# The first norm of a two-layer backbone: x in two halves between the modulation tiles, ten tiles on TensorE, squares added by VectorE

## The reference

```python
def rms_norm(x, g):
    xf = x.astype(F32)
    y = xf * lax.rsqrt(jnp.mean(xf * xf, axis=-1, keepdims=True) + EPS)
    return (y * g.astype(F32)).astype(x.dtype)

def _modulate(h, g, m, k):
    return (rms_norm(h, g) * (1 + m[:, :, 3 * k + 1]) + m[:, :, 3 * k]).astype(h.dtype)

def _half_ffn(h, g, m, k, w1, w3, w2):
    y = swiglu(_modulate(h, g, m, k), w1, w3, w2)
    return h + (0.5 * m[:, :, 3 * k + 2] * y).astype(h.dtype)
```

## Time and profile before

| | us |
|---|---|
| median of three timed runs | 2786.47 |
| the profiled execution | 2784.83 |
| its span | 2783.1 |
| TensorE busy | 2675.1 (96%) |
| VectorE busy | 2056.2 (74%) |
| ScalarE busy | 1176.3 (42%) |
| GpSimd busy | 390.2 (14%) |

### The profile page before, as it was taken

The page is one execution under the profiler, slowest core; times in us unless marked ns, Lnnn a source line. Parts: engine busy times, 40 slices in busy tenths (PEclk is TensorE's granted clock), DMA queues, the critical chain, the costliest instruction groups (busy, mean ns, idle before and its releaser), DMA issues.

```text
span 2783.1 us, 40131 instructions
## 1 busy us (share of the span) xinstructions
PE 2675.1 (96%) x15624; PEld 2512.6 (90%) x15624; DVE 2056.2 (74%) x3184; ACT 1176.3 (42%) x1860; POOL 390.2 (14%) x312
## 2 busy tenths in 40 slices
PE   5999999999988999999999999999999989999999
PEld 5999999998976899999999999999997775788898
DVE  7887878774558587878777877787878667666674
ACT  3233333346447644332323523242436866533342
POOL 3111111110012521111111211100022410211000
PEclk8999999999999999999999999999999999999999
DMA  9888989621120047889897589874522110378453
GB/s 347 209 228 248 274 252 267 169 67 54 59 62 1 1 143 203 245 224 281 229 274 212 137 221 258 248 214 131 165 69 83 61 46 1 114 201 235 145 165 125
DMA packets 161691, 464.13 MB, mean 167 GB/s; under 512 B 13281, under 2 KB 14433, under 8 KB 160609
## 3 DMA queue, kind: packets, MB, share of 16 engines
q1 hardware_dynamic: 87200, 247.65, 26.3%
q0 software_dynamic: 56448, 146.81, 24.3%
q10 hardware_dynamic: 17856, 67.12, 6.8%
HBM read 459.43 MB, written 148.90 MB: 219 GB/s over the span
## 4 chain that ended last, share of the span: by engine, by line
PE 78%; DVE 11%; DMA 5%; ACT 3%; issue 3%; POOL 0%; ACTq 0%; SPq 0%; DVEq 0%; POOLq 0%
PE banks L698 11%; PE banks L702 11%; PE banks L700 11%; PE banks L786 9%; PE banks L788 9%; PE banks L787 9%; DMA raw<-sums 4%; PE banks L705 3%; PE banks L709 3%; PE banks L707 3%; DVE banks L2019 1%; DVE tmp L2292 1%; PE banks L1233 1%; DVE wl L2086 1%; DVE wl L2014 1%
## 5 line engine op out<-in xcount | busy, mean ns | idle before, releaser
L1362 ACT ACTIVATE wh<-raw 128x1024 fp32r<-128x1024 f32 (+2 forms) x194 | 181.8, 937 | 611.8 <-PE banks L702 458.7
L2019 DVE SCALAR_TENSOR_TENSOR banks<-mraw,scb 128x1024 f32<-128x1024 f32 x240 | 304.9, 1270 | 11.6 <-DMA mraw<-in_wmn 7.9
L2014 DVE TENSOR_TENSOR wl<-raw,wh 128x1024 fp32r<-128x1024 f32 (+2 forms) x216 | 234.3, 1085 | 95.5 <-ACT wh L1362 93.2
L1427 ACT ACTIVATE wh<-raw 128x512 fp32r<-128x512 f32 (+1 forms) x210 | 161.6, 774 | 326.6 <-DMA raw<-sums 156.7
L698 PE MATMUL banks<-hh,wh 128*128 128x384 f32 x1056 | 270.4, 337 | 9.3 <-DVE wl L2014 9.0
L786 PE MATMUL banks<-xh,wh 128*128 128x384 f32 (+1 forms) x796 | 258.0, 324 | 12.8 <-DVE wl L2086 12.7
L702 PE MATMUL banks<-hh,wl 128*128 128x384 f32 x1056 | 269.9, 336 | 0.0
L700 PE MATMUL banks<-hl,wh 128*128 128x384 f32 x1056 | 269.7, 336 | 0.0
L788 PE MATMUL banks<-xh,wl 128*128 128x384 f32 (+1 forms) x796 | 256.6, 322 | 0.0
L787 PE MATMUL banks<-xl,wh 128*128 128x384 f32 (+1 forms) x796 | 256.5, 322 | 0.0
L698 PE MATMUL banks<-xh,wh 128*128 128x384 f32 x880 | 230.7, 343 | 21.4 <-DVE xl L2284 12.0
(11 more groups left out here) (427 smaller groups left out, 6225.5 us busy)
## 6 DMA issues: line engine op xcount, KB each, us to landing
raw<-sums SPq DMA_DIRECT2D x140, 512.0 KB, 6.0
sums<-in_w POOLq DMA_DIRECT2D x88, 768.0 KB, 8.5
mraw<-in_wmn ACTq DMA_DIRECT2D x120, 512.0 KB, 5.7
a<-in_w SPq DMA_DIRECT2D x70, 512.0 KB, 4.3
sums<-in_w POOLq DMA_DIRECT2D x22, 1536.0 KB, 8.8
sums<-sums POOLq DMA_DIRECT2D x44, 768.0 KB, 9.6
raw<-in_w SPq DMA_DIRECT2D x80, 384.0 KB, 4.3
raw<-in_w SPq DMA_DIRECT2D x52, 512.0 KB, 3.9
```

The costliest lines, as they stand in the source:

```text
L1362: act.activation(wh[slot][:, 0:nk * P], raw[slot][:, 0:nk * P], ACT.Copy).then_inc(hi_done, 1)
L1427: act.activation(W_HI[slot_of(name, last)], W_SRC[name], ACT.Copy).then_inc(w_hi, 1)
L2014: dve.tensor_tensor(wl[slot][:, 0:nk * P], raw[slot][:, 0:nk * P], wh[slot][:, 0:nk * P].bitcast(F32), ALU.subtract).then_inc(lo_done, 1)
L2019: return dve.scalar_tensor_tensor(B67[:], tile, 1.0, scv[:, s, :], ALU.mult, ALU.mult, accum_out=out)
```

## The change

SyncE loads par, the first two weight tiles and scb0, then the minis in eight groups with x in two halves behind the first and the second group. The scale tiles (8 to 15) come first, then the shift tiles. TensorE makes ten minis (8 to 12, then, behind the sum of the squares, 0, 1, 2, and once rstd is there 4 and 5), VectorE six (13, 14, 15, 3 ahead of the norm; 6 and 7 inside it, between the fourth `scaled` and `rest(0)`). ScalarE writes eight squares into eight buffers, with no wait between them; VectorE adds them to one sum, so the sum over partitions is two matmuls and not four. The bias is added in three batches: scale, shift of chunks 0 to 3, shift of chunks 4 to 7; ScalarE's xh(0) and xh(4) wait for the second and third. The splits of the first two weight tiles move to the front of ScalarE's and VectorE's programs. The gate tiles are issued behind weight tiles 2 and 3, each once the minis in its place are read. GpSimd's chain of DMAs waits for the last mini.

```diff
-PE_MINI = (1, 3, 5, 7, 9, 11, 13)
-DVE_MINI = (0, 2, 4, 6, 8, 10, 12, 14, 15)
-MINI_GROUPS = ((0, 1, 2), (3, 4, 5, 6), (7, 8, 9, 10), (11, 12, 13), (14, 15))
+PE_MINI = (8, 9, 10, 11, 12, 0, 1, 2, 4, 5)
+DVE_MINI = (13, 14, 15, 3, 6, 7)
+MINI_GROUPS = ((8, 9, 13), (10, 11, 14), (12, 15), (3, 0), (6, 1), (7, 2), (4,), (5,))
...
+            def load_gate_minis():
+                for q in range(2):
+                    sp.wait_ge(mini_mm, 2 + q)
+                    sp.wait_ge(mini_dot, (9, 14)[q])
+                    sp.dma_start(gmini[q][:], dr["wmn"][16 + 4 * q:20 + 4 * q].rearrange("t p n -> p t n")).then_inc(gmini_landed, 16)
+                sp.dma_start(wdt[:], dr["wdt"]).then_inc(gmini_landed, 16)
...
+            for q, js in enumerate(MINI_GROUPS):
+                for j in js:
+                    src = dr["wmk"][PE_MINI.index(j)] if j in PE_MINI else dr["wmn"][j]
+                    sp.dma_start(mini[j][:], src).then_inc(mini_landed[q], 16)
+                if q < 2:
+                    half_k = slice(4 * q, 4 * q + 4)
+                    sp.dma_start(x[:, half_k, :], dr["x"][:, half_k, :]).then_inc(x_landed[q], 16)
...
             for j in PE_MINI:
-                if j == 11:
-                    pe.wait_ge(con_landed, 16)
+                if j == 0:
+                    pe.wait_ge(x_landed[0], 32)
                     norm_sums(0, SEGS)
+                if j == 4:
+                    pe.wait_ge(rstd_ready, 1)
...
                 for j in range(KC):
+                    if n == 0 and j % 4 == 0:
+                        act.wait_ge(mini_dot, (9, 14)[j // 4])
                     act.wait_ge(v_ready, 8 * n + j + 1)
...
+            def add_square(j):
+                dve.wait_ge(sq_done, j + 1)
+                if j > 1:
+                    dve.wait_ge(ssq_acc, j - 1)
+                dve.tensor_tensor(ssq[:], ssq[:], squares[j][:], ALU.add).then_inc(ssq_acc, 1)
...
+            def shift_batch(q):
+                dve.wait_ge(mini_mm, 2 + q)
+                dve.wait_ge(mini_dot, (8, 13)[q])
+                first_bias(4 * q, (3, 2)[q], 4).then_inc(mini_dot, 1)
+                dve.wait_ge(mini_dot, (9, 14)[q])
+
+            def first_between(q):
+                if q == 0:
+                    shift_batch(0)
+                    first_dots(6, 9)
+                    first_dots(7, 11)
+                if q == 1:
+                    shift_batch(1)
...
-            add_squares(0, T)
+            pool.wait_ge(mini_landed[len(MINI_GROUPS) - 1], 16 * len(MINI_GROUPS[-1]))
```

More of the change, by code:

```diff
@@ L277, in pr @@
             return par[:, PCOL[n][0]:PCOL[n][1]]
-        mini = [at(f"mini{j}", [P, D], XH + j * D) for j in range(2 * KC)]
-        gmini = [at("gmini0", [P, 4, D], H + 4 * D), at("gmini1", [P, 4, D], H)]
+        mini = [at(f"mini{j}", [P, D], (H if j < KC else XH - KC * D) + j * D) for j in range(2 * KC)]
+        gmini = [at(f"gmini{q}", [P, 4, D], H + 4 * q * D) for q in range(2)]
+        squares = [ssq, sq[0], sq[1], tmp[0], tmp[1], tmp[2], tmp[3], rstd]
         scb0 = at("scb0", [P, 2, D], HID + 2 * HC * T - 3 * T)
@@ L623, in load_ffn @@
                             load(t0 + 2 * i + 1, src[1], KC)
+                        if (f, g, i) == (0, 0, 1):
+                            load_gate_minis()
                     row2 = KC * W2_ROW[f, g]
@@ L633, in load_ffn @@
                             load_a2(f, g + 1, 0)
+            def load_gate_minis():
[4 more added lines that the diff above has]
+                sp.dma_start(wdt[:], dr["wdt"]).then_inc(gmini_landed, 16)
             sp.dma_start(par[:], dr["par"]).then_inc(par_landed, 16)
+            for s in range(2):
+                sp.dma_start(raw[s][:, 0:D], dr["w13"][s]).then_inc(raw_landed[s], 16)
             sp.dma_start(scb0[:], dr["ccb"]).then_inc(scb_landed, 16)
[L637 to L651, removed]
+            for q, js in enumerate(MINI_GROUPS):
[6 more added lines that the diff above has]
+                if q == 0:
+                    sp.dma_start(con[:], dr["con"]).then_inc(x_landed[0], 16)
             load_ffn(0)
@@ L749, in norm_sums @@
                 pe.wait_ge(ssq_acc, 7 * (n + 1))
+                if n == 0:
+                    for a, b, _s in segs:
+                        mm = pe.matmul(NP[:, a:b], cst("ones"), ssq[:, a:b], start=True, stop=True)
+                    mm.then_inc(norm_sum, 1)
+                    return
                 for a, b, _s in segs:
@@ new lines, in shift_batch @@
+            def shift_batch(q):
[4 more added lines that the diff above has]
+            def first_between(q):
+                if q == 0:
+                    shift_batch(0)
[3 more added lines that the diff above has]
+                    shift_batch(1)
+            chain(dve.memset(eps[:], EPS))
@@ L2860, in _ @@
+            split_lo(0, 0, KC)
+            split_lo(1, 1, KC)
+            dve.wait_ge(scb_ready, 1)
+            first_dots(13, 0)
+            for j in range(1, 4):
+                add_square(j)
+            first_dots(14, 2)
+            for j in range(4, KC):
+                add_square(j)
+            first_dots(15, 4)
+            first_dots(3, 6)
             dve.wait_ge(par_landed, 16)
             dve.wait_ge(mini_mm, 1)
-            dve.wait_ge(mini_dot, 2 * len(DVE_MINI))
-            pairs = G[0][:, 0:4 * KC].rearrange("p (t s) -> p t s", s=2)
@@ L2864, in _ @@
-            for js, src in ((slice(1, 14, 2), pairs), (slice(0, 15, 2), M), (slice(15, 16), M)):
-                n_ = len(range(16)[js])
-                chain(dve.tensor_tensor(M[:, js, :], src[:, js, :], pr("bmod")[:, js].unsqueeze(2).to_broadcast([P, n_, 2]),
-                                        ALU.add))
+            dve.wait_ge(mini_dot, 8)
+            chain(first_bias(KC, 5, KC))
             prep(0)
-            norm(0, SEGS, lambda s: None)
+            norm(0, SEGS, first_between)
```

62 lines of the change are left out of this document (33 added, 29 removed).

## The result

The changed kernel took 2793.89 us (median of 20 runs, 2785.42 to 2807.29), the kernel before 2787.11 beside it (20 runs, 2780.5 to 2790.54): a ratio of 1.0025, 95% interval 1.0016 to 1.0033. It is slower by about 7 us; the prediction was 2785.1, with 2790.0 as its upper end. Run again on another chip the ratio was 1.0035 (1.0022 to 1.0048). The profiled execution took 2795.98 us (span 2794.2, mean granted clock 0.991; before 0.990).

What follows compares the result with a forecast made beforehand. Bound taken: a chain of waits (first minis landing, VectorE's 18 dots, the norm) up to TensorE's first large product at 57.09 us. Sum: -5.8 + 2.7 + 1.7 = -1.4 against 2786.47, so 2785.1 us; range 2779.5 to 2790.

Steps and rivals of the forecast that it cites:

- The time to the first product: TensorE's start on its first large product: 51.3 us where it was 57.09, so 5.8 us won.
- the formula: Landing times of the first loads: 3.3 + 1.225 n us, with n counted in minis of 512 KB.
- the lower level: TensorE's clock at 1.2 GHz during minis, 3.45 us each; the upper level is 2.4 GHz.
- the new wait of VectorE: In the norm, after four `scaled`: VectorE waits from 41.4 us for TensorE's mini 2 at 44.35.
- rival C: Minis behind the sum of the squares run at 1.9 us: start 48.4, 8.7 won, 2782.2 us; chance 10%.
- what is late next: Behind the first product: scb, slowed by the second gate load, lands at 70.4, silu 72.3, after TensorE's 69.6.
- a stall of 2.7: TensorE waiting for scb's silu behind its first large product: 2.7 us, bounds 0 to 5.5.
- 1.7 for the clock: Behind TensorE's stop of 5.1 us the granted clock falls to 0.50 for some 3 us: 1.7 us lost.
- rival D: scb and second gate load meet, but worse: stall 6.9, clock 2.4, +3.5 us, 2790.0 us; chance 18%.
- TensorE waiting later for sums: A sign in the profile after that would make the prediction wrong; no size was given.
- the dots with the gate tiles: Gate tiles land about 71 to 73 us, needed by VectorE's dots at 74.7: just hidden.
- GpSimd's chain ahead of the second norm: GpSimd's DMAs start at 36.8 and not 31.3 us, leaving 8 of 15.9 us to spare: hidden.

Runs made afterwards that it cites:

- e1: The changed kernel with scb's load issued right behind rstd's Exp and not behind xh(7): ratio 0.9981 to the kernel before.
- e5: The changed kernel unaltered, run again on another chip: ratio 1.0035 to the kernel before.
- e8: The changed kernel with scb loaded right behind rstd's Exp and GpSimd's chain started behind the fourth group of minis: ratio 0.9996 to the kernel before.
- e10: The changed kernel with scb loaded right behind rstd's Exp and the second gate load issued behind weight tile 4: ratio 0.9983 to the kernel before, 2785.6 us.
- e11: The changed kernel with scb loaded right behind rstd's Exp, measured once more: ratio 0.9990 to the kernel before, 2785.28 us.
- e2: The changed kernel with GpSimd's DMA chain started when the fourth group of minis has landed, not the last: ratio 1.0002 to the kernel before.
- e6: The changed kernel with the second gate load and wdt issued behind weight tile 4: ratio 1.0009 to the kernel before, 2789.85 us.
- e4: The kernel before with three more tiles in `wmk` that nothing reads, shifting later tensors in DRAM: ratio 1.0004 to the kernel before.
- e9: The kernel before with ScalarE copying scb onto itself twice ahead of its silu: ratio 1.0015 to the kernel before.
- e3: The kernel before with GpSimd's DMA chain started only when the last mini has landed: ratio 0.9982 to the kernel before.
- e7: The kernel before with scb's load issued right behind rstd's Exp: ratio 0.9991 to the kernel before unaltered.
- e12: The kernel before with scb's load issued right behind rstd's Exp, measured once more: ratio 0.9987 to the kernel before unaltered, 2784.06 us.

## Why the prediction was wrong

**The time to the first product was right.** Predicted 51.3, measured 51.96 (and 51.3 to 52.0 in e1, e5, e8, e10 and e11). The two groups and the two halves of x on TensorE's path landed 0.6 to 1.0 us behind the formula (the last minis, which nothing on the path waits for, by up to 2); the minis behind the sum of the squares took 17.07 / 5 = 3.41 us each, the lower level, as taken; rstd was there at 38.1 (predicted 37.1); the new wait of VectorE was 2.53 us. 5.1 us won, 5.8 predicted. The two executions e2 and e6 show that rival C can happen in part: there the first product came at 49.83 and 49.45, where C, its sum put right (41.8 + 5.3 + 1.1 is 48.2), has 48.2.

**The step that failed is "what is late next".** It gave scb 8.0 us, a stall of 2.7 and 1.7 for the clock, and of the other neighbour it said "GpSimd's DMA chain lies beside it as it did before". Three things are wrong in that. And the sum has no term at all for the rounds that read the sums; more on that below.

First, the size: scb took 9.2 us, the stop grew by 4.6 (6.04 - 1.42), and the low clock of 6.05 us behind it took 3.0. Set against the start (5.1) and the shorter low clock behind the first product (1.5 us lost there where it was 2.5), that is 4.6 + 3.0 - 5.1 - 1.0 = 1.5 us lost, and the split is 1.3 late. The mechanism is rival D's, which was to decide from a stall of 4.1 us; 4.6 was measured. The 8.0 had been taken as the middle between 5.3 and 10.8 (by its own terms, 5.3 and half of 11.6, the upper one is 11.1), with no row in which two such loads lie together. And the first product does not end at 75.36, where ScalarE gets its buffer back, but at 76.31 (77.73 less the wait of 1.42): the stop before was 1.42 us and not 2.4. The forecast's 5.1 us of stop are 4.1 by this measure, and 6.04 were measured.

Second, the neighbour. I took the second gate load as what makes scb slow. But e4 and e9 had 8.6 and 9.3 us with no gate load near, and e6 still 7.5 without it; e10 against e11 shows no gain in moving it, though e10 pays for that elsewhere. With scb behind the norm, the six executions in which GpSimd's transfer was issued 1.3 us or more ahead of it had 7.5 to 9.3 us, the two with less than that 4.8 and 5.3. The gate load may add up to 1.7 us in the new order (9.2, 8.8 and 8.9 against 7.5), but it isn't needed. That it is the transfer is read from which loads lie together in eight executions; of edits, only e3 moves the transfer alone, in the old order, where scb was quick already. The changed kernel with that one transfer held back until scb has landed was not run. In the kernel before it was issued 0.68 us ahead:

```profile
65.84 1.26 POOL L2916 DMA_DIRECT2D sums<-in_w  x1 [11.62 <-issue]
```

With its own issue at 66.52, its profile showed the good case. The rates fit: from scb's issue to 68 us and from there to 70 the core's DMAs moved 26 and 159 GB/s in e4 (busy for 65% and 96%), and 74 and 340 (53% and 83%) in the kernel before. So it looks as if the slow DRAM to DRAM transfer was served first in e4 and scb in the kernel before. The changed order issues scb 3.6 us earlier, into the middle of the transfer issued at 57.50, each time that it was profiled. The Trainium skill (DMA: Bandwidth & Descriptors, Queues, rings and completion order) has each DMA engine go round-robin between the queues that have work. The trace of the changed kernel agrees in kind: scb and the transfer both finish late, after 9.2 and 15.8 us, where in e10, with neither scb nor the second gate load beside it, the same transfer took 7.6. I had applied the rule to SyncE's queue alone.

Third, the kernel before seems to pay this toll too, in some of its executions: e4, whose program is the same but for tiles that nothing reads, showed it. e3, which moves the transfer behind scb (0.7 us), and e7 and e12, which move scb away, are 0.9982, 0.9991 and 0.9987 of it, but only e3's interval ends below 1. How often it happens no run shows. That the one profile of a kernel with two ways to go may have drawn the good one was no part of my range.

**Is the late scb the cause?** For the sign, taking it away is enough: the one edit that does so turns 1.0025 and 1.0035 into 0.9981 and 0.9990, and the intervals do not touch. The same edit in the old order (e7, e12) is worth a quarter of that. Of the gain the profiles show 6.2 us at the split (131.1 against 137.3: restart 3.5 us earlier, the low clock gone). But it isn't shown to be the only cause: e6 and e2 took 6 to 9 us off the changed kernel by the ratios, with scb still at 7.5 and 8.9 us and stops of 4.3 and 5.8. Nor can the other low stretches of the changed kernel be put down to the late scb. The one at 140 us follows a stop of 2.88 us that the kernel before has too, with the same low stretch behind it, as have e7 and e12, where scb is early; e1, e8 and e11 have the stop and stay at the full clock. The one at 318 us is missing in e5 and there in e12 (near 321).

**What stays open** is the later part, and it decides the forecast: with only the 1.5 us of the failed step, the prediction's own sum would have given 2788.0, inside its range; the measured 2793.89 lies outside by what comes after 137 us. The prediction put that part at nothing, without a row, and named "TensorE waiting later for sums" as a sign that it is wrong; that sign is there. By the medians the change costs 6.8 us; 1.3 are there at 137 us in one execution, and -1.3 in another (e5). The rest is in the rounds that read the sums, where TensorE's waits come to 18.6 and 15.2 us in the changed kernel, 12.7 before. The chain's start (against it e3 and e8, for it e2), the DRAM places (e4) and the stop itself (e9: 7.2 us of such waits after the longest stop of all) don't explain it by themselves. e10 had 17.3 us of them with no late scb, though with late gate tiles, and ended 10.9 us behind before; e11 had 12.3. They differ from execution to execution of one kernel, and fourteen profiles do not say by what. Nor is it clear why a lead of 5 us at 131 us (e11 against e12: 131.1 and 136.1), which is still there at the end of the two profiled executions (2780.5 and 2785.8), isn't seen in the medians (2785.28 and 2784.06). No run here holds the later waits fixed.

**What was hidden as predicted.** The first squares and rstd; `shift_batch(1)`; the dots with the gate tiles, which began at 76.12, right behind tile 2's rest and with no wait; GpSimd's chain ahead of the second norm, which answers to the earlier trace rows:

```profile
544.99 1.40 POOL L2945 COPY ssq<-sq 128x768 f32<-128x768 f32 x1 [7.55 <-ACT sq L1497]
```

Early by 7.6 us where 8 were predicted and 15.9 stood before.

## What to carry to other kernels

A step that is started earlier moves every transfer behind it as well: look up each one's neighbours at its *new* time, on every queue, GpSimd's among them, and not only the neighbour that the change itself moves. If a small load stands on the path and its data and buffer are there long before, issue it early: the rebuilt start was worth nothing that shows without it, and with it no more than the old start with the same edit (e1 and e11 against the changed kernel: 10 to 15 us by the ratios; e7 and e12 against the kernel before: about 3, with intervals that end at 1.0002). A cure that moves another load needs the same look: e6 and e10 made VectorE wait for the gate tiles. And where the profiled time of a load hangs on which of two issues comes first by under a microsecond, take both times into the range.

## What the runs showed of the hardware

- A load of 1 MB behind the norm took 4.8 and 5.3 us, or 7.5 to 9.3 where GpSimd's queue had been given its transfer more than a microsecond earlier. Between 0.7 us ahead (5.3) and 1.3 us (8.6) lies the whole step, on two executions. GpSimd's instruction that issues the transfer lasted 1.26 us: in the first it was still running when scb was issued, in the second it had just ended. That this order decides fits all eight, but was not tested, and e7's early load, 0.5 us behind a transfer and with other loads about it, took 7.2, so the bound is not a rule.
- With stops of 3.7 to 8.4 us of TensorE behind its first large product a low granted clock came every time (3.4, 6.8 or 10.2 us long, begun within the stop in five of the six), and with the 1.42 us at the same place never. Its length does not follow that of the stop alone: 6.04 us went with 6.8 us of it, 5.71 with 3.4. A stop of 2.88 us some 60 us later was followed by a low stretch in ten of the thirteen executions that have it, and in e1, e8 and e11 by none; nothing here says why.
- The price of a stop is not only itself: in e9 7.0 us more of stop made 9.8 us at the split, 2.4 of them by the low clock behind it.
- Matmuls with 2 columns stayed at the lower level for 17 us in a row (80 of them, 17.07 us). In two of the eight executions of the new order (e2 and e6) the first of them behind the sum of the squares ran at the upper one, until 39 us.
- Profiled executions of nearly the same work ended at 2776.4 and 2785.8 us (e7 and e12), 2778.2 and 2780.5 (e1 and e11), 2794.2 and 2789.0 (after and e5). A difference of 5 us between two single profiles says nothing about the kernel; the same instruction at 76 or 137 us does, within 0.6 us at the split (130.99 and 131.10; 135.47 and 136.06) where no clock or load went the other way. Among 35 timed runs of the kernel before on one chip the times went from 2777.88 to 2800.1 us.
